# Streamed layer kernel: order of SyncE's loads, pace of the last weight change, and two additions moved from GpSimd to VectorE

## The reference

```python
h = rmsnorm(x, g_pre); p = h @ w_in + b_in
q_a, k_a, v_a, z_a, q_m, k_m, v_m, o_m, z_m, i_m, f_m, g_a, g_b = split(p)
att = sliding_window_attention(q_a, k_a, v_a, sinks)        # window 128, 16 meta tokens
hm  = mlstm_chunkwise(q_m, k_m, v_m, i_m, f_m, state)        # 4 heads of width 256
y_a = att * silu(z_a);  y_m = sigmoid(o_m) * hm * silu(z_m)
merged = sigmoid(g_a) * (y_a @ w_pa) + sigmoid(g_b) * (y_m @ w_pb)
y = x + rmsnorm(merged @ w_out, g_post)
```

## Time and profile before

| | us |
|---|---|
| median of 3 runs (lowest, highest) | 2826.03 (2825.18, 2828.23) |
| the profiled execution, its own time | 2831.79 |
| its span in the trace | 2830.0 |
| mean granted clock | 0.988 of full speed |
| attention stage | 0 to 857 |
| the ten passes | 860.8 to 2819.2 |
| last product to the end | 10.8 |

### The profile page before, as it was taken

The page is one execution under the profiler, slowest core; times in us unless marked ns, Lnnn a source line. Parts: engine busy times, 40 slices in busy tenths (PEclk is TensorE's granted clock), DMA queues, the critical chain, the costliest instruction groups (busy, mean ns, idle before and its releaser), DMA issues. The chain is left out here.

```text
span 2830.0 us, 46426 instructions
## 1 busy us (share of the span) xinstructions
PE 2735.1 (97%) x15620; PEld 2287.2 (81%) x15620; DVE 1642.1 (58%) x4145; ACT 939.0 (33%) x2291; POOL 702.4 (25%) x1022
## 2 busy tenths in 40 slices
PE   6999999999999999999999999999999999999898
PEld 5888888888887867787887887888887888788786
DVE  5776665555663245465556546556337662577887
ACT  5774443444441021132122113114123231333533
POOL 3333533533551022202212222221100000022222
PEclk9999999999999999999999999999999999999999
DMA  8664566555767898888889888898896577957634
GB/s 316 236 219 159 173 200 208 170 181 168 228 221 259 280 339 279 289 271 291 292 270 301 283 283 292 265 291 279 290 328 218 197 266 248 325 191 242 212 149 149
DMA packets 410526, 697.47 MB, mean 246 GB/s; under 512 B 31778, under 2 KB 177575, under 8 KB 410260
## 3 DMA queue, kind: packets, MB, share of 16 engines
q1 hardware_dynamic: 298724, 526.72, 56.2%
q10 hardware_dynamic: 108848, 158.46, 16.4%
q0 software_dynamic: 2720, 9.32, 1.0%
HBM read 526.87 MB, written 169.48 MB: 246 GB/s over the span
## 5 line engine op out<-in xcount | busy, mean ns | idle before, releaser
L2847 PE MATMUL bank_second<-w_all,a_all 128*128 128x512 f32 x736 | 299.7, 407 | 12.2 <-DMA a_all<-hh_t 8.3
L2850 PE MATMUL bank_second<-w_all,a_all 128*128 128x512 f32 x736 | 289.5, 393 | 0.0
L2849 PE MATMUL bank_second<-w_all,a_all 128*128 128x512 f32 x736 | 288.9, 392 | 0.0
L2430 ACT ACTIVATE mx_qkt<-st_bank_t 128x512 f32<-128x512 f32 x68 | 40.8, 600 | 570.8 <-PE st_bank_t L2870 562.7
L2847 PE MATMUL bank_first<-w_all,a_all 128*128 128x512 f32 x496 | 200.2, 404 | 11.7 <-DMA a_all<-hh_t 3.9
L2850 PE MATMUL bank_first<-w_all,a_all 128*128 128x512 f32 x496 | 195.1, 393 | 0.0
L2849 PE MATMUL bank_first<-w_all,a_all 128*128 128x512 f32 x496 | 194.5, 392 | 0.0
L2847 PE MATMUL bank_third<-w_all,a_all 128*128 128x512 f32 x464 | 188.5, 406 | 4.3 <-DMA a_all<-sh_t 3.0
L308 PE MATMUL bank_first<-w_all,a_all 128*128 128x384 f32 x536 | 186.5, 348 | 0.0
L2850 PE MATMUL bank_third<-w_all,a_all 128*128 128x512 f32 x464 | 181.2, 390 | 0.0
L2849 PE MATMUL bank_third<-w_all,a_all 128*128 128x512 f32 x464 | 180.8, 390 | 0.0
(11 more groups left out here) (404 smaller groups left out, 7251.0 us busy)
## 6 DMA issues: line engine op xcount, KB each, us to landing
a_all<-sh_t SPq DMA_DIRECT2D x224, 512.0 KB, 5.4
a_all<-hh_t SPq DMA_DIRECT2D x180, 512.0 KB, 5.7
a_all<-hh_t ACTq DMA_DIRECT2D x104, 512.0 KB, 4.9
h_raw<-l_blocks_in ACTq DMA_DIRECT2D x64, 512.0 KB, 5.9
difs_t<-h_raw ACTq DMA_DIRECT2D x64, 512.0 KB, 6.6
st_waiting<-difs_t SPq DMA_DIRECT2D x118, 256.0 KB, 6.5
st_waiting<-l_blocks_in SPq DMA_DIRECT2D x84, 256.0 KB, 6.2
hh_t<-a_all SPq DMA_DIRECT2D x34, 512.0 KB, 6.0
```

The source lines that it names most:

```text
L2847: T.matmul(bank_view(bank, at), hi, weight_row(k, at, 0, t), start=fresh and t == 0, stop=False, skip_group_check=True)
L2849: T.matmul(bank_view(bank, at), hi, weight_row(k, at, 1, t), start=False, stop=False, skip_group_check=True)
L2850: last = T.matmul(bank_view(bank, at), lo, weight_row(k, at, 0, t), start=False, stop=t == KH - 1, skip_group_check=True)
```

## The change

Six edits, all in the order or the place of existing work; no arithmetic is added or dropped.

1. The sample mask's transfer is counted on order_in instead of c_in. The sink matmul waits for three counts of c_in instead of four; the sample masks' user waits for three of order_in instead of two.
2. `unit_split_at` for OUT's pieces: -6 + 2x//5 instead of -6 + x//3, so that piece 27 comes four turns into the pass instead of three; its load (two turns before) and its low half (one after) move with it.
3. `mixers_of` loads the gate and decay rows two turns ahead instead of four.
4. In SP's turn `next_operand` comes before `load_unit`.
5. PB's addition of PA's result (17 rows) and OUT's addition of x (17 rows), 128x1024 each, move from POOL to DVE, the first right behind the row's scaling (`merge_row`), the second right behind its norm. POOL keeps `load_pa`.
6. In OUT, P2's copy out of the bank (8 of them) moves from DVE to ACT.

```diff
--- before.py
+++ after.py
@@ -632,7 +632,7 @@
             load_xt(2)
             store_h(0)
             sp.dma_start(smask[:, :, :], k.c_smask).then_inc(order_in, 16)
-            sp.dma_start(amask[:, :, :], k.c_amask).then_inc(c_in, 16)
+            sp.dma_start(amask[:, :, :], k.c_amask).then_inc(order_in, 16)
             sp.dma_start(perm[:, :, :, :], k.c_perm).then_inc(order_in, 16)
             load_x(3)
             store_h(1)
@@ -1274,7 +1274,7 @@
             def sample_masks(a):
 
                 n0, d0 = PE_N * a, DVE_N * a
-                dve.wait_ge(order_in, 16 * 2)
+                dve.wait_ge(order_in, 16 * 3)
                 for i in range(2):
                     dve.wait_ge(smp_pe, n0 + 2 + i)
                     V.tensor_tensor_reduce(out=ssm[:, i, :], in0=p_s[i][:, 0:3 * P], in1=smask[:, i, :], scale=1.0,
@@ -1426,7 +1426,7 @@
             first_block(p_b[:, 0:W + GATES], attn_base(0) + ZC, W + GATES, k.AT[0] + 2, lambda: pe.wait_ge(gate_lo, 1)).then_inc(proj_b, 1)
             first_block(p_a[:, 0:ZC], attn_base(0), ZC, k.AT[0] + 5, lambda: scale_row(1)).then_inc(proj_a, 1)
             scale_row(2)
-            pe.wait_ge(c_in, 16 * 4)
+            pe.wait_ge(c_in, 16 * 3)
             T.matmul(p_s[1][:, 0:KVH], headrow, sink4[:, :], start=True, stop=True).then_inc(sink_done, 1)
 
             def gate_transposed(m):
@@ -1781,7 +1781,7 @@
     s, x = v // N_UNIT, v % N_UNIT
     if s == 0:
         return -3 if x < EARLY + KH else 5 + (x - EARLY - KH) // 2
-    return N_PROD * s - 6 + (x // 3 if s >= PA else x // 2)
+    return N_PROD * s - 6 + (x * 2 // 5 if s == OUT else x // 3 if s >= PA else x // 2)
 
 
 def unit_lowered_at(v):
@@ -2156,7 +2156,7 @@
                     sp.dma_start(lmask[:, :, :], k.c_lmask).then_inc(const_in[0], 16)
                     sp.dma_start(seqpair[:, :], k.c_seqpair).then_inc(const_in[1], 16)
                     load_states(0)
-                n = TURN.get(q + 4)
+                n = TURN.get(q + 2)
                 if n is not None:
                     load_z(n)
                     if n >= 2:
@@ -2193,10 +2193,10 @@
                     sp.dma_start(k.o_p_n[0, 0], nrow[NB * MH:, :]).then_inc(state_out, 16)
 
             for q in range(-4, Q_ALL + 8):
+                if 6 <= q + LOADED_AHEAD < Q_ALL:
+                    next_operand(q + LOADED_AHEAD)
                 for v in LOADS_AT.get(q, ()):
                     load_unit(v)
-                if 6 <= q + LOADED_AHEAD < Q_ALL:
-                    next_operand(q + LOADED_AHEAD)
                 if q < 0:
                     continue
                 s, x = q // N_PROD, q % N_PROD
@@ -2284,18 +2284,8 @@
 
                 if row >= len(tile_rows(g)):
                     return
-                s, at = g // N_ITEM, line_of(g, row)
-                if s == PB:
-                    n = row_turn((PB,), g, row)
-                    pool.wait_ge(scaled[row], row_turn(SCALING, g, row))
-                    pool.wait_ge(e_in[2 + row], 16 * n)
-                    G.tensor_tensor(c[:, at, 0:D], c[:, at, 0:D], e[:, 2 + row], ALU.add).then_inc(merged[row], 1)
-                    if n < N_ITEM - row:
-                        load_pa(g + 1, row)
-                elif s == OUT:
-                    pool.wait_ge(normed, tile_rows(g)[row] + 1)
-                    pool.wait_ge(e_in[row], 16 * row_turn(SCALING, g, row))
-                    G.tensor_tensor(e[:, row], c[:, at, 0:D], e[:, row], ALU.add).then_inc(scaled[row], 1)
+                if row_turn((PB,), g, row) < N_ITEM - row:
+                    load_pa(g + 1, row)
 
             G.memset(eps, EPS).then_inc(eps_set, 1)
             for v in LOWERS_AT[-3]:
@@ -2305,7 +2295,7 @@
             for q in range(Q_ALL + 8):
                 for row in range(2):
                     g = ended(q - 1 - 2 * row, row)
-                    if g is not None and g // N_ITEM in (PB, OUT):
+                    if g is not None and g // N_ITEM == PB:
                         finish(g, row)
                 if q == N_PROD * PB:
                     for row in range(2):
@@ -2476,6 +2466,10 @@
                         act.wait_ge(prod, q)
                         act.wait_ge(c21_ready, m)
                         A.activation(t1[:, :], bank_x[:, :], ACT.Copy).then_inc(t1_ready, 1)
+                    if i and j == P2 and s == OUT:
+                        act.wait_ge(prod, q)
+                        wait_line(act, N_ITEM * s + i, 0, 0)
+                        A.activation(c[:, 0, 0:LW], bank_x[:, :], ACT.Copy).then_inc(c11_ready, 1)
                 if q + DIF_LEAD in DIF_NOW:
                     load_dif(DIF_NOW[q + DIF_LEAD])
                 if q - DIF_LEAD in DIF_NOW:
@@ -2531,6 +2525,13 @@
                 V.scalar_tensor_tensor(out=c[:, line_of(g, row), cols], in0=e[:, row, cols], scalar=1.0, in1=c[:, line_of(g, row), cols],
                                        op0=ALU.add, op1=ALU.mult).then_inc(scaled[row], 1)
 
+            def merge_row(g, row):
+
+                at, n = line_of(g, row), row_turn((PB,), g, row)
+                dve.wait_ge(scaled[row], row_turn(SCALING, g, row))
+                dve.wait_ge(e_in[2 + row], 16 * n)
+                V.tensor_tensor(c[:, at, 0:D], c[:, at, 0:D], e[:, 2 + row], ALU.add).then_inc(merged[row], 1)
+
             def wait_bias(s):
                 if s == ZM:
                     dve.wait_ge(k.first_bias_in, 16)
@@ -2560,6 +2561,8 @@
                         dve.wait_ge(c11_ready, g + 1)
                         dve.wait_ge(c12_ready, g + 1)
                         dve.sem_inc(scaled[0], 1)
+                        if s == PB:
+                            merge_row(g, 0)
 
             def evict_pair(g, j):
                 s, m = g // N_ITEM, pairs_before(g)
@@ -2586,9 +2589,7 @@
                     wait_line(dve, g, 0, 0)
                     if s in STREAMED:
                         V.tensor_tensor(c[:, 0, 0:LW], bank_x[:, :], bias_of(s)[:, 0:LW], ALU.add).then_inc(c11_ready, 1)
-                    elif s == OUT:
-                        V.tensor_copy(c[:, 0, 0:LW], bank_x[:, :]).then_inc(c11_ready, 1)
-                    else:
+                    elif s != OUT:
                         dve.wait_ge(e_in[0], 16 * row_turn(SCALING, g, 0))
                         V.scalar_tensor_tensor(out=c[:, 0, 0:LW], in0=e[:, 0, 0:LW], scalar=1.0, in1=bank_x[:, :],
                                                op0=ALU.add, op1=ALU.mult).then_inc(c11_ready, 1)
@@ -2641,6 +2644,9 @@
                 dve.wait_ge(rstd_ready, n)
                 V.scalar_tensor_tensor(out=c[:, at, 0:D], in0=c[:, at, 0:D], scalar=rstd[:, row:row + 1], in1=gpost,
                                        op0=ALU.mult, op1=ALU.mult).then_inc(normed, 1)
+                dve.wait_ge(normed, n)
+                dve.wait_ge(e_in[row], 16 * row_turn(SCALING, g, row))
+                V.tensor_tensor(e[:, row], c[:, at, 0:D], e[:, row], ALU.add).then_inc(scaled[row], 1)
 
             def weighted(n):
 
@@ -2777,6 +2783,8 @@
                 if g is not None and g // N_ITEM in (PA, PB):
                     wait_whole(dve, g, 1)
                     scale_row(g, 1, slice(0, D))
+                    if g // N_ITEM == PB:
+                        merge_row(g, 1)
                 for row in range(2):
                     g = ended(q - 2 - 3 * row, row)
                     if g is not None and g // N_ITEM == OUT:
```

## The result

The changed kernel is slower: 2841.91 us in the median of 10 runs (2834.30 to 2846.84), against 2824.62 for the kernel before in 10 runs beside it (2822.64 to 2828.23). The ratio is 1.0056, 95% interval 1.0043 to 1.0068, so by the ratio +15.8 us (12.1 to 19.2; the two medians lie 17.3 apart). The forecast was 2818.8 with a range to 2830. The profiled execution took 2842.8 us, its span is 2841.0; before it was 2830.0.

What follows compares the result with a forecast made beforehand. PE, busy 97% of the span, was taken as the bound, with some 50 us of waits and half clock reachable. The terms summed to -7.2 us, from a median of 2826.0 to 2818.8 us; 8-in-10 range 2806 to 2830.

Steps and rivals of the forecast that it cites:

- Sink matmul: At L1430: no longer waits for the mask, but the transposes behind still wait for DVE's sinks; 0 us, at most 0.3.
- Operands first into PA, PB: At GA's and GB's ends: PE's gaps go, DVE's chain binds next; -2.5 us into PA, -1.2 into PB.
- GB's start: GB's first five products: operands issued ahead of pieces bring them from 15.45 to 13.6 us, -1.85.
- H0's start: At H0's start: the last pieces land later behind the operand's 0.52 MB; +1.0 us (0 to +3).
- Starts of H1 to GA: Starts of H1 to GA: pieces have room, tightest 0.9 us in H2, so later pieces cost 0 us.
- Rival C: Head passes: pieces issued late behind the operand's slot wait cost 3.8 us at each of four changes; 2834 us, chance 0.09.
- Operand 88: H0's product 28: operand issued and landing 3.6 us earlier, so PE's gap and the slow clock behind shrink; -4.8 us.
- Products 35 and 36: H0 to H2, beside the state loads: next step's rows now fall there, 0.8 us each, three times; +2.4 (0 to +4).
- DVE's additions: PB's pairs: last row's addition comes ahead of L2578, losing PE 0.2 to 0.3 us in 7 pairs; +1.75 (0 to +3).
- OUT's start: OUT's first products: fewer lowerings before the single's copy, but pieces 25 to 27 on the chain; -0.3 us (-5 to +3).
- The end: OUT's last row: norm and addition of 1.25 us each on DVE, limited by x's load; -1.7 us (-3 to -1).
- all differences carry over: Final sum: differences from the profiled execution, 5.8 us above the median, apply unchanged to the median 2826.0; gives 2818.8 us.

Runs made afterwards that it cites:

- the combination: Kernel before plus window copies in PA, spread state loads, rows two turns ahead, operands first at GA's/GB's ends, DVE additions, ACT copy, late low halves: 2804.95 us.

## Why the prediction was wrong

Its own steps in order.

- **Sink matmul, 0:** right. L1430 no longer waits (3.3 us before), but the transposes at L1534 now wait 1.68 us for DVE's sinks instead of 0.27 and start at 32.40 us, 32.74 before. ZM begins at 858.8 us, within 854.2 to 860.8 of kernels that kept the wait.
- **Operands first into PA, PB:** the mechanism was right. The waits went and DVE's chain took their place: the kernel with this order at the two ends alone shows -6.7 and +2.5 at GA and PA, -7.4 and +2.1 at GB and PB, against the profiled execution. I had 2.5 and 1.2 us of gain there; by that trace it is 4.2 and 5.3. Yet that kernel's median is no lower. The 7.5 us at GA were one execution's, 1.9 is the middle of the seven others; the 4 us that this leaves are not seen in the runs, and whether they are there is open.
- **GB's start, -1.85:** wrong. The first five products took 0.5 us more; in the three kernels with operands first there they take 15.95 to 17.3 us, in the eleven others 14.6 to 15.45. The DMA engines are full there (1.04 in rows 4), and another order of the same bytes brought no gain; I had taken the order for the cause.
- **H0's start, +1.0 (0 to +3):** mis-sized, 34.0 us for the first eight products against 29.7, +4.2. I also misread the place: before, PE waits there 1.9 us for pieces but 4.2 for operands as well, and the clock, 1.00 before, fell to 0.90. I counted only the operand's bytes ahead of the last pieces, and not the wait that every turn's pieces now stand behind, nor that this lateness feeds itself.
- **Starts of H1 to GA, 0:** this step failed outright. I asked for the slack of the pieces that PE uses soon (0.9 us) and found enough. But +2.6, +2.2, +2.2 and +1.1 us were lost at products 8 and 9 through pieces 26 and 27, used 14 us later: ACT is in order, it waits for the piece's landing, and the mixer's copy is behind it; DVE stands for the same piece with its evictions behind it. I never listed what is queued behind the waiting instruction on ACT and DVE. Products 0 and 6 of H2 and H3 lost 1.9 us more. Rival C had the right edit, side and places, at 0.09, but the wrong mechanism (PE waiting for pieces) and a size of 3.8 each: 2834, where 2841.9 was measured.
- **Operand 88, -4.8:** right, -4.4. Counted from the start of product 23 it is issued 2.6 us earlier instead of 3.6, it still lands only 14.3 us later, and PE's wait for it is down to 0.2 us.
- **Products 35 and 36, +2.4 (0 to +4):** right place, mis-sized: +5.0 in H0 and +1.8 in H1, in the kernel with edit 3 alone 5.5 and 3.6. I priced the rows' bytes (0.8 us) and not that the operand is issued behind the rows and 6.7 us of state loads and takes 1.4 us longer to land, nor that a gap so long brings the half clock behind it. I also took the 4.7 us of waits in rows 3 for this place; 3.9 of it stand in ZM and at H0's start, and behind the state loads PE waited 1.0, 1.3 and 2.3 us, for hh_t operands into bank_first. H2 shows nothing against the one profile, but 2 to 3 us against a usual execution.
- **DVE's additions, +1.75:** right, and slightly small: 0.35 us a pair instead of 0.25, in six pairs instead of seven, 2.1 us. L2520, now L2514, is at 0.69 us in OUT, where rows 9 had 1125 ns:

```profile
L2514 DVE TENSOR_TENSOR a_all<-h_raw,a_all 128x512 fp32r<-128x512 f32 x21 | 14.4, 685 | 4.1 <-ACT a_all L2325 4.1
```

  The Trainium skill (SBUF — State Buffer, SBUF: two separate sides) has this as the exclusive lock between DVE and GpSimd, and the trace agrees. It changed no time in OUT's steady part, whose products take 2.72 us before and after: nothing waited for DVE there.
- **PB's start:** not seen. Besides P7's bank, PE waited 2.3 us for the first row that DVE scales (L2806 for L2533): the transposes of PB's result hang on the same chain. It is edit 4's, not the additions': with operands first alone, POOL still adding, the wait for the same row is 3.0 us, and with the additions alone there is none.
- **OUT's start, -0.3:** +0.2, the gain at products 3 to 5 (3.4 us) and the loss at 6 and 7 (4.0) both as described.
- **The end, -1.7:** -1.6, 10.8 to 9.2 us. Norm and addition follow each other at once:

```profile
2835.33 1.28 DVE L2645 SCALAR_TENSOR_TENSOR st_c<-st_c,st_small,st_e 128x1024 f32<-128x1024 f32 x1
2836.65 1.23 DVE L2649 TENSOR_TENSOR st_e<-st_c,st_e 128x1024 f32<-128x1024 f32 x1
```

Set against each other, by the two traces: the gains forecast came true (the two ends, operand 88, the last row), 20 us of them, and PA and PB took back 7.2 where I had given them 12.4. What was missed are 8.2 us at H1 to GA's starts and 1.9 more in H2 and H3, 3.2 at H0's start, 4.4 at products 35 and 36, 2.3 at GB's start and 0.5 at OUT's. With ZM's 4.6 and the attention stage's -2.0 that turns -7.2 into about +11. ZM's part is no loss of the change: kernels that leave ZM's order alone are +2.0 to +4.5 against the same execution.

The last 5 us lie in the step "all differences carry over". I took them from an execution 5.8 us above its median (7.2 above the median of ten), and 5 to 6 us at GA's end and 2 to 3 at H2's products 35 and 36 were in that execution and not in a usual one. What a median doesn't hold can't be taken out of it.

## What to carry to other kernels

Before moving a load behind another one that waits on the consumer's progress, list for every engine what is queued behind its wait for that load: a piece with 14 us of slack at its user still cost 2 us, because an in-order engine stood before it with urgent work behind. Read the price of a burst by the time it holds the issuing queue and by the clock behind the gap, and not by its bytes alone. And take a stall from more than one execution before counting on its removal: here 7.5 us stood in one and 0.9 to 4.8 in seven others, while removing two bursts of issues that had nothing to do with the change gave 10 us and the combination 24.

## What the runs showed of the hardware

Executions of the same kernel spread over 12 us (2819.7 to 2831.8 in 25 of before), and between traces the wait for one and the same transfer differs by several us (GA's end: 0.9 to 7.5 us lost in eight traces). Where the DMA share stands at 1.04, issuing the same bytes in another order did not shorten the stretch (GB's start: 14.6 to 15.45 us in eleven kernels, 15.95 to 17.3 in the three with operands first). And one addition of 128x1024 took DVE 1.23 us, where POOL had taken 2.0 to 2.6; DVE's subtractions of 128x512 took 1.13 us in the mean beside it and 0.69 without it.
